# Two transformer blocks on one core: attention scores over all 128 rows, last chunks in halves, activations ahead of casts, steps set back, and products of constants at two borders

## The reference

```python
def first_block(x, c, positions, ...):                      # one layer
    mod = c_act @ ada_w + ada_b                             # six vectors: shift, scale, gate, twice
    h = rmsnorm(x, g) * (1 + scale_m) + shift_m
    x = x + gate_m * token_mix(h, ...)                      # p = h @ w_in; GLA and MLA; @ gla_wo, @ mla_wo, @ w_out
    h = rmsnorm(x, g2) * (1 + scale_f) + shift_f
    x = x + gate_f * ((silu(g) * u) @ w_down)               # g, u = split(h @ ffn_w_in)
    return rmsnorm(x, final_g)

def mla_attention(q_nope, q_rope, k_nope, k_rope, v):       # 16 heads; nope 128 wide, rope 64 wide
    s = q_nope @ k_nope.T + q_rope @ k_rope.T               # k_rope is the same for all heads
    return softmax(mask(s * scale)) @ v

def second_block(x, ...):                                   # two layers
    for l in range(2):
        rq, rk, rv, rg, dq, dk, dv, dg, lx, lg = split(rms_norm(x) @ w_in[l])
        # retention (6 heads), differential attention (4 heads, two score maps c = 0, 1, each 64 wide), gated LRU
        y = concat(ret_out, diff_out, lru_out) @ w_out[l]
        x = x + rms_norm(y, post_g)
    return x
```

## Time and profile before

| | |
|---|---|
| median of three runs | 2684.96 us (2682.71 to 2686.86) |
| the profiled execution, its time | 2684.43 us |
| its span in the profile | 2681.9 us |
| PE busy | 2581.6 us, 96% |
| PEld (weight loads of PE) busy | 2179.1 us, 81% |
| DVE busy | 1718.7 us, 64% |
| ACT busy | 1303.7 us, 49% |
| POOL busy | 74.4 us, 3% |
| mean of HBM reads and writes | 206 GB/s |
| mean granted clock of TensorE | 0.992 |

### The profile page before, as it was taken

One profiled execution on the slowest core, in us unless ns is written; L12 is line 12 of the kernel. 1 busy time (PEld: TensorE's weight loads), 2 busy tenths in 40 slices (PEclk: granted clock), 3 DMA queues, 4 the chain that ended last, 5 costly groups with the idle time before them and its releaser, 6 DMA issues.

```text
span 2681.9 us, 35445 instructions
## 1 busy us (share of the span) xinstructions
PE 2581.6 (96%) x12959; PEld 2179.1 (81%) x12959; DVE 1718.7 (64%) x2260; ACT 1303.7 (49%) x1897; POOL 74.4 (3%) x110
## 2 busy tenths in 40 slices
PE   3989999999999998999999999999999999999999
PEld 3878887888787887888888888889887887888886
DVE  6877876776666755677655555566656655565664
ACT  3344555434455444544443444455654545564553
POOL 0000000000000000000000000002000101100000
PEclk9999999999999999999999999999999999999999
DMA  9975665887675765677766666666465464555464
GB/s 363 347 241 157 190 202 174 302 295 254 197 252 183 231 208 180 226 263 263 229 196 194 184 185 185 188 189 194 146 186 166 143 210 142 174 170 176 144 202 133
DMA packets 325062, 554.25 MB, mean 207 GB/s; under 512 B 24462, under 2 KB 135804, under 8 KB 324252
## 3 DMA queue, kind: packets, MB, share of 16 engines
q1 hardware_dynamic: 319104, 541.79, 63.7%
q0 software_dynamic: 3168, 7.12, 0.8%
q10 hardware_dynamic: 2620, 3.09, 0.3%
HBM read 549.83 MB, written 2.10 MB: 206 GB/s over the span
## 4 chain that ended last, share of the span: by engine, by line
PE 86%; issue 5%; DVE 4%; ACT 3%; DMA 1%; SPq 0%; POOL 0%; DVEq 0%; POOLq 0%; ACTq 0%
PE gp L816 78%; PE tp L816 6%; PE tp L819 2%; DMA raw_first<-in_ada_w_dram 1%; ACT whi L1238 1%; DVE wlo L1848 1%; DVE acc L1854 0%; ACT hraw L1238 0%; ACT L1238 0%; DVE xs L1848 0%; SPq L799 0%; DVE yd L1848 0%; ACT h L1238 0%; DVE acc L1848 0%; ACT mxh L1238 0%
## 5 line engine op out<-in xcount | busy, mean ns | idle before, releaser
L1848 DVE TENSOR_TENSOR wlo<-raw,whi 128x1024 fp32r<-128x1024 f32 (+1 forms) x830 | 983.6, 1197 | 651.0 <-ACT whi L1238 647.6
L1238 ACT ACTIVATE whi<-raw 128x1024 fp32r<-128x1024 f32 (+1 forms) x830 | 848.9, 1036 | 610.0 <-PE gp L816 489.4
L816 PE MATMUL gp<-whi,h 128*128 128x512 f32 (+1 forms) x2944 | 926.7, 387 | 4.5 <-DVE wlo L1848 3.0
L816 PEld LDWEIGHTS gp<-whi,h 128*128 128x128 f32 x2944 | 551.8, 189 | 109.4 <-issue 12.2
L816 PE MATMUL gp<-h,whi 128*128 128x512 f32 (+1 forms) x1936 | 602.8, 371 | 25.6 <-DVE wlo L1848 11.5
L816 PE MATMUL gp<-wlo,h 128*128 128x512 f32 (+1 forms) x1472 | 561.5, 381 | 0.0
L816 PE MATMUL gp<-h,wlo 128*128 128x256 f32 x1680 | 473.5, 282 | 0.0
L816 PEld LDWEIGHTS gp<-h,whi 128*128 128x128 f32 x1936 | 352.2, 191 | 96.6 <-issue 20.4
L816 PEld LDWEIGHTS gp<-h,wlo 128*128 128x128 f32 x1680 | 319.9, 190 | 0.8 <-issue 0.7
L816 PEld LDWEIGHTS gp<-wlo,h 128*128 128x128 f32 x1472 | 278.0, 189 | 44.9 <-issue 1.0
L1854 DVE SCALAR_TENSOR_TENSOR acc<-raw,cact,acc 128x1024 f32<-128x1024 f32 x149 | 190.5, 1279 | 7.7 <-DMA raw<-in_ada_w_dram 7.0
(11 more groups left out here) (329 smaller groups left out, 2636.3 us busy)
## 6 DMA issues: line engine op xcount, KB each, us to landing
raw<-in_w_in_dram SPq DMA_DIRECT2D x310, 512.0 KB, 4.3
raw<-in_ffn_w_in_dram SPq DMA_DIRECT2D x176, 512.0 KB, 4.6
raw<-in_ada_w_dram SPq DMA_DIRECT2D x158, 512.0 KB, 5.0
raw<-in_w_out_dram SPq DMA_DIRECT2D x96, 512.0 KB, 4.3
raw<-in_ffn_w_down_dram SPq DMA_DIRECT2D x88, 512.0 KB, 4.3
raw<-in_w_in_dram SPq DMA_DIRECT2D x64, 384.0 KB, 3.5
raw_first<-in_ada_w_dram SPq DMA_DIRECT2D x34, 512.0 KB, 7.9
raw<-in_gla_wo_dram SPq DMA_DIRECT2D x32, 512.0 KB, 5.5
```

The lines of the kernel that those rows point to most:

```text
L816: return e.matmul(o, l, r, start=start, stop=stop)
L1238: return e.activation(o, i, f, **kw)
L1848: return e.tensor_tensor(o, a, b, op)
```

## The change

Seven edits, all in the order or the form of work on tiles that exist already.

1. `pr_sc` and, for heads 0 and 1, `df_S` multiply over all 128 rows. For this `krt` becomes two tiles, one for each head, with the key in one half and zeros in the other, and `dkt` gets a second tile in the same way. POOL writes the zeros; ACT copies each half by itself. Heads 2 and 3 of `df_S` stay as they are.
2. The last chunk of the jobs `xo` 3, `w2` (0, 3) and `w2` (1, 3) runs over both tiles of its contraction for tokens 0 to 127 first, then for tokens 128 to 255, and a new semaphore, `mm_half`, lets the evacuation of the first half start six products before the end.
3. Ahead of the first unit of `fg` 0, `rvg` (1, 0), `gk` and three jobs `q`, `make_timeline` now steps the stages through the activations of the first two chunks before it puts the next prep. (For the three jobs `q` the order stays as it was.)
4. Steps are set back: in `pair` the part `pr_kn` and the part `pr_rr` come one step later; `dq`, `dk` and `rqk` end with an idle step, so that `diff` and `ret` start one unit later.
5. `ada_add` does both of its halves in its first step.
6. The addition of the first 512 columns of x at the border of the two layers goes in two halves of 256, and the first transpose waits for the first half.
7. `warm`: eight products of the identity with 256 constant columns on PE ahead of the transposes of `ffn`, and four ahead of those of `lend`. Nobody reads them.

```diff
+HALVES = [("xo", 3), ("w2", 0, 3), ("w2", 1, 3)]
+BORDERS = [("fg", 0), ("rvg", 1, 0), ("q", 0, 0), ("q", 0, 1), ("q", 0, 2), ("gk",)]
...
-        return [idle, step(("ada_add", (seq, 0), 0)), step(("ada_add", (seq, 1), 0)), idle, step(("ada_out", (seq, 0), 1)), step(("ada_out", (seq, 1), 1))]
+        return [step(("ada_add", (seq, 0), 0), ("ada_add", (seq, 1), 0)), idle, idle, idle, step(("ada_out", (seq, 0), 1)), step(("ada_out", (seq, 1), 1))]
...
-        return [step(("pr_rope", (p,), 0), ("pr_qn", (p,), 1), need=before), step(("pr_kn", (p,), 1)), step(("pr_rr", (p,), 1)), idle,
+        return [step(("pr_rope", (p,), 0), ("pr_qn", (p,), 1), need=before), idle, step(("pr_kn", (p,), 1)), step(("pr_rr", (p,), 1)),
...
+            first = [("f_rn", (), 0), ("warm", ("hf", 0), 1), *[("f_sc", (n,), 0) for n in range(4)]] if pair == 0 else []
...
-            [step(("rp_T", (kind, l, j, k), 1)) for k in (0, 2)]
+            [step(("rp_T", (kind, l, j, k), 1)) for k in (0, 2)] + [idle]
...
+            a = [("le_rn", (l,), 0), ("warm", ("h1", 0), 1), ("le_add", (l, 0), 0)] if j == 0 else []
...
+        if job["name"] in BORDERS and ci == 0:
+            for k in job["order"][0:2]:
+                for kk in range(job["kn"]):
+                    until(*stat_need(job, k + kk))
...
+        def warm(us, stat, j):
+            (u,) = us
+            bk = empty(u)
+            for n in range(4 if stat == "h1" else 8):
+                last = mm(bk[:, 0:S], ident, cst[:, C_ID:C_ID + S], True, True)
+            last.then_inc(tp_full[u.b], 1)
...
-                last = mm(bk[:, c0:c0 + n], QRT[r0:r0 + 64, t * P:(t + 1) * P], KRT[r0:r0 + 64, 0:n], False, True)
+                last = mm(bk[:, c0:c0 + n], QRT[:, t * P:(t + 1) * P], KRT[h][:, 0:n], False, True)
...
+            w.wait_ge(x_add, at("x_add", 0, pair // 2) if pair else 2)
...
-            bk, r0 = empty(u), 64 * c
+            bk, rows = empty(u), slice(0, P) if h < 2 else slice(64 * c, 64 * c + 64)
+            w.wait_ge(dk_zero, 2 * (l + 1))
...
-                last = mm(bk[:, c0:c0 + n], DQT[r0:r0 + 64, h, t * P:(t + 1) * P], DKT[r0:r0 + 64, h, 0:n], True, True)
+                last = mm(bk[:, c0:c0 + n], DQT[rows, h, t * P:(t + 1) * P], DKT[c if h < 2 else 0][rows, h, 0:n], True, True)
...
+                split = job["name"] in HALVES and ci == len(job["chunks"]) - 1
+                for kk, t in ((0, 0), (1, 0), (0, 1), (1, 1)) if split else ((0, 0), (0, 1), (1, 0), (1, 1)):
                     k = 2 * ci + kk
                     hh, hl = stationary(job, job["order"][ci] + kk)
-                    for t in range(2):
-                        o, tk = gp[2 * g + t][:, 0:N], slice(t * P, (t + 1) * P)
-                        mm(o, hh[:, tk], WHI[:, slot, kk, 0:N], k == 0, False)
-                        mm(o, hh[:, tk], WLO[:, slot, kk, 0:N], False, False)
-                        last = mm(o, hl[:, tk], WHI[:, slot, kk, 0:N], False, k == K - 1)
+                    o, tk = gp[2 * g + t][:, 0:N], slice(t * P, (t + 1) * P)
+                    mm(o, hh[:, tk], WHI[:, slot, kk, 0:N], k == 0, False)
+                    mm(o, hh[:, tk], WLO[:, slot, kk, 0:N], False, False)
+                    last = mm(o, hl[:, tk], WHI[:, slot, kk, 0:N], False, k == K - 1)
+                    if split and (kk, t) == (1, 0):
+                        last.then_inc(mm_half, 1)
...
+            bk = full(u)
+            for h in range(2):
+                r = slice(64 * h, 64 * h + 64)
+                copy(KRT[h][r, :], bk[r, 0:S]).then_inc(tp_act[u.b], 1)
...
+            if job["name"] in HALVES:
+                w.wait_ge(mm_half, HALVES.index(job["name"]) + 1)
+            else:
+                w.wait_ge(mm_done, job["chunks"][-1]["w"] + 1)
...
+            for cj in (slice(0, 256), slice(256, 512)) if (l, j) == (0, 0) else (cj,):
+                for n in range(2 if l == 0 else 1):
+                    stt(X[:, n, cj], Y[:, n, cj], scol(2, "le_rs", l)[:, n:n + 1], X[:, n, cj], ALU.mult, ALU.add).then_inc(x_add, 1)
...
+        def gk_krt(us):
+            w.wait_ge(hi_done, first_w)
+            w.wait_ge(lo_done, first_w)
+            w.wait_ge(ada_dve, 4 * KD)
+            for h in range(2):
+                e.memset(KRT[h][64 - 64 * h:128 - 64 * h, :], 0.0).then_inc(krt_zero, 1)
+                w.wait_ge(krt_zero, h + 1)
+        def rp_T(us, kind, l, j, k):
+            if kind == "dk" and k == 0:
+                w.wait_ge(rope_done, at("rope", kind, l, j))
+                for c in range(2):
+                    e.memset(DKT[c][64 - 64 * c:128 - 64 * c, 0:2, :], 0.0).then_inc(dk_zero, 1)
+                    w.wait_ge(dk_zero, 2 * l + c + 1)
```

More of the change, by code:

```diff
@@ L355, in stage_steps @@
         for pair in range(8):
-            first = [("f_rn", (), 0), *[("f_sc", (n,), 0) for n in range(4)]] if pair == 0 else []
+            first = [("f_rn", (), 0), ("warm", ("hf", 0), 1), *[("f_sc", (n,), 0) for n in range(4)]] if pair == 0 else []
             ahead = [("f_sc", (n,), 0) for n in (pair + 3, pair + 4) if pair in (1, 3)] + ([("f_gfb", (), 0)] if pair == 7 else [])
@@ L603, in program @@
     mxg_hi, mxg_lo, rope_done, ret_scale, ret_gate = (sem(n) for n in ("mxg_hi", "mxg_lo", "rope_done", "ret_scale", "ret_gate"))
-    df_max, df_exp, df_mix = (sem(n) for n in ("df_max", "df_exp", "df_mix"))
+    df_max, df_exp, df_mix, krt_zero, dk_zero = (sem(n) for n in ("df_max", "df_exp", "df_mix", "krt_zero", "dk_zero"))
     values, counts = {}, {}
@@ L980, in pr_sc @@
             (u,) = us
-            bk, r0 = empty(u), 64 * h
+            bk = empty(u)
+            w.wait_ge(krt_zero, 2)
             for part in ("pr_qn", "pr_kn", "pr_rr"):
@@ L1029, in le_T @@
         def le_T(us, pair):
-            w.wait_ge(x_add, at("x_add", 0, pair // 2))
+            w.wait_ge(x_add, at("x_add", 0, pair // 2) if pair else 2)
             x_T(us[0], pair)
@@ L1412, in gk_krt @@
             first_read()
-            copy(KRT[:, :], full(u)[:, 0:S]).then_inc(tp_act[u.b], 1)
+            bk = full(u)
+            for h in range(2):
+                r = slice(64 * h, 64 * h + 64)
+                copy(KRT[h][r, :], bk[r, 0:S]).then_inc(tp_act[u.b], 1)
             note(tp_act[u.b], "tpa", *u)
@@ L1687, in evac @@
                 return
-            w.wait_ge(mm_done, job["chunks"][-1]["w"] + 1)
+            if job["name"] in HALVES:
+                w.wait_ge(mm_half, HALVES.index(job["name"]) + 1)
+            else:
+                w.wait_ge(mm_done, job["chunks"][-1]["w"] + 1)
             ps = [gp[2 * g], gp[2 * g + 1]]
@@ L1793, in evac @@
                 for n in range(2):
+                    if n:
+                        w.wait_ge(mm_done, job["chunks"][-1]["w"] + 1)
                     if j or n:
@@ L2430, in le_add @@
                 w.wait_ge(x_add, at("x_add", 0, j))
-            for n in range(2 if l == 0 else 1):
-                stt(X[:, n, cj], Y[:, n, cj], scol(2, "le_rs", l)[:, n:n + 1], X[:, n, cj], ALU.mult, ALU.add).then_inc(x_add, 1)
+            for cj in (slice(0, 256), slice(256, 512)) if (l, j) == (0, 0) else (cj,):
+                for n in range(2 if l == 0 else 1):
+                    stt(X[:, n, cj], Y[:, n, cj], scol(2, "le_rs", l)[:, n:n + 1], X[:, n, cj], ALU.mult, ALU.add).then_inc(x_add, 1)
             note(x_add, "x_add", l, j)
```

19 lines of the change are left out of this document (10 added, 9 removed).

## The result

The changed kernel takes 2658.16 us (median of 4 runs, 2657.15 to 2658.97), beside 2685.43 for the kernel before in the same measurement. The ratio is 0.9899, with a 95% interval from 0.9882 to 0.9917: 1.0% faster. The forecast was 2657 in a range from 2648 to 2669. Its total is right; the terms for the scores and for the clock are not, and they largely cancel.

The account below looks back on a forecast made before the run. TensorE, busy 96% of the span, was taken to bound the kernel. Terms of 15.4, 7.8, 0.9, 1.0, 3.0 and 0.7 sum to 28.8; less 1.5 returned, 27.3 off 2684.43 gives 2657 us, range 2648 to 2669.

Parts of the forecast that it names:

- Scores over 128 rows: `pr_sc` and `df_S` of heads 0 and 1: padding removes changes of rows, 12.6 and 2.8 us, together 15.4.
- I take 1.5: Deduction from the summed gain: TensorE, faster where casts feed it, gives 1.5 us back as waits for `whi` or `wlo`.
- rival C: TensorE waits for ACT and VectorE: `qrt` waits doubled, a third of the scores' gain returned; 2666 us, chance 0.14.
- Waits: Steps set back remove waits for `acc`, `kv`, `dkt`, `rqk`, `mxl`, 10.2 us, less 2.4 for new `qrt` waits: 7.8.
- `gk`: Third pair of tiles no longer waits for the low part of `h`, as a cast goes behind: 0.9 us.
- rival E: Slower: padded products or shifted waits make the clock fall where it did not; 2689 us, chance 0.03.
- Feed-forward border: Border into the feed-forward part: halves and a later cast save 1.3 us, less what returns at the eighth pair: 1.0.
- Layer border: Between the layers: halves, split additions, later casts and a clock likely held save 3.0 us, bounds 1.7 and 3.6.
- three chances in four that it holds: Layer border: chance given that the clock stays at full speed, behind the 3.0 us term.
- the falls I know come behind 5 us: Layer border: clock falls follow about 5 us of idle time, so 2.3 us of idle should likely hold it.
- End: Last job: evacuation in halves starts as much sooner as at the layer border, 0.7 us, bounds 0 and 0.8.
- rival D: Clock gives more: it holds at both borders and one or two falls within work go; 2649 us, chance 0.07.

Follow-up runs that it names:

- e3: Kernel before with each `pr_sc` block's products sorted by rows, two changes of rows instead of four, no padding: 2679.91 us, ratio 0.9976.
- e2: Changed kernel with the scores over 64 rows again; zeros, second copies and order stay: 2670.41 us, ratio 0.9938 to the kernel before.
- e1: Kernel before with only the padding of the scores to 128 rows added: 2674.41 us, ratio 0.9963.
- e5: Changed kernel with edits 4 and 5 undone (steps not set back, `ada_add` late again): 2668.35 us, ratio 0.9932 to the kernel before.
- e4: Changed kernel without the products of constants (`warm`) at both borders: 2660.95 us, ratio 0.9904 to the kernel before.
- e12: Changed kernel with the two heads' scores of a pair two steps apart instead of one: 2652.58 us, ratio 0.9872 to the kernel before.
- e13: e12 with the `warm` edit of e10: 2652.82 us, ratio 0.9877 to the kernel before.
- e10: Changed kernel with eight products of constants, not four, at the layer border and four more ahead of `qk`'s wait: 2655.84 us, ratio 0.9893 to the kernel before.

## Why the prediction was right, by its steps

**Scores over 128 rows, 15.4.** The mechanism and the block were right: 0.78 a block against 0.79, 0.39 against 0.35 for `df_S`, and 0.19 for a change of rows, shown by e3. What failed is the price of what comes back, "I take 1.5". In the pairs 5.7 to 6.4 us of the 12.5 came back (e2, e1), 3.3 to 4.1 of them as waits mostly for `wlo`. This is the half of rival C that lets 5 us of the scores' gain return; its other half, the waits for `qrt` doubled, did not come, and it named the cause only in general. The busy shares of ACT and DVE, which I held against C, say nothing here: each engine waits for the other in the chain.

**Waits, 7.8.** e5 gives 10.2 by the medians and 9.2 by the starts of the same products. Its trace has two falls of 1.7 more and one of 1.7 less, so 7.5 to 8.5 for the waits. The three new waits for `qrt` took 2.2 (forecast 2.4). That the sum is right is in part luck: the new waits for `sx` (1.3) and `rg` (1.5 more) were missing from it, and so was the gain of 0.8 at `sg`; and of the 2.8 for `acc` the longest, 1.3 at 1199, gave nothing that lasted.

**`gk`, 0.9.** 1.1 measured, and then 1.7 lost at 264 in the clock, which only rival E had in general, with a chance of 0.03.

**Feed-forward border, 1.0.** The first unit came 2.3 us sooner, 0.6 of it was left by 1197. About 0.9 went by the path described: ACT has little room over the eight pairs of tiles, and `h` is waited for three times, not twice. The rest went in the slower pace of the products told of above. The clock held there, and e4 shows that nothing of this lasted.

**Layer border, 3.0.** 1.8 measured, near the lower bound of 1.7, since the clock fell after all. The two halves gave their 1.25; the 0.4 by the casts is not there (TensorE waits 1.21 us for `h`, before 1.15). The 5.22 us of the earlier trace rows are idle time of the weight loads; TensorE itself waited 4.80, and now 1.82. In the three traces in which the clock held (e5, e12, e13) the border gives 3.3, so that both ends of the term were sound and its chance was not: "three chances in four that it holds" was too high, since of the ten traces with the products it held in three. The step behind it failed, "the falls I know come behind 5 us": those at 599 and 691 came behind waits of 0.40 and 0.22 us. The products made the fall shorter (1.7 against 5.1 by the windows of e4). By the page "TensorE: Matmul & The Clock Gate" of the Trainium skill, Part 1, being busy releases the throttle. At the other border the clock held in eight of the ten traces with eight products; here it fell in seven of ten, in e10 with eight products too, so that at this border the runs do not bear it out.

**End, 0.7.** 0.4 measured, since TensorE had waited only 0.24 us for `diag`.

**The clock inside work.** Only rival D had it, with a chance of 0.07. Three falls went and one came: 3.4 us gained. So, against the forecast's 27.3: 4.3 to 5.0 us less in the pairs, 1.2 less at the layer border and 0.7 less at the other border and the end; 3.4 more by the clock, 0.5 more by `df_S` and `gk`, 0.9 more at the start by chance, and between 0.3 less and 0.7 more by the waits. That makes 24.9 to 26.6, beside 25.1 of span and 27.3 by the medians. The mechanisms of the scores and of the waits were right; the total was right through errors that cancel, which is luck.

## What to carry to other kernels

Compare small products by the column, with neighbours of the same kind: where products over 64 and over 128 rows take turns, filling up with zeros or sorting them by rows takes off the changes. Before counting such a gain, look for a chain that goes back and forth between two engines in the same stretch and measure its period, here 4.62 us from one `wlo` to the next: if a step of TensorE comes below it, the rest returns as waits, however idle both engines are. And look at the granted clock behind every wait, not only behind the long ones.
